# Layer four's attention: the fourth query unit is multiplied before the keys are turned, and its evacuation and squares move with it

## The reference, cut to what matters

```python
z = h @ w_in
cq = rms_norm_2(z[..., :o1], q_norm_g)
ckv = rms_norm_2(z[..., o1:o2], kv_norm_g)
q = (cq @ w_q_up).reshape(b, s, MLA_HEADS, QK_DIM)
kv = (ckv @ w_kv_up).reshape(b, s, MLA_HEADS, NOPE_DIM + V_DIM)
...
q = rms_norm_2(q, qn_g)
k = rms_norm_2(k, kn_g)
q = jnp.concatenate([q[..., :NOPE_DIM], rope(q[..., NOPE_DIM:], positions)], axis=-1)
k = jnp.concatenate([k[..., :NOPE_DIM], rope(k[..., NOPE_DIM:], positions)], axis=-1)
o = causal_block_attention(q, k, v)
...
mem_out = memory_attention(q_mem, mem_k, mem_v, mem_qn_g[i], mem_kn_g[i])
x = x + jnp.concatenate([mix, mem_out], axis=-1) @ w_out
```

## Time and profile before

| what | value |
|---|---|
| median of 3 runs | 1572.5 us (1572.43 to 1573.7) |
| the profiled execution's own time | 1575.78 us |
| its span | 1574.0 us, granted TensorE clock 0.98 on the mean |
| PE, DVE, ACT busy | 95%, 84%, 66% of the span |
| chain that ended last | PE 70%, DVE 20%, ACT 4% of the span |

### The profile page before, as it was taken

How to read it: one execution, slowest core, us unless ns; L and a number is a source line. 1 busy time by engine, 2 the same in 40 slices (tenths; PEclk the granted TensorE clock), 3 DMA queues, 4 the chain that set the end, 5 groups by cost and what they waited for, 6 DMA issues and landing times.

```text
span 1574.0 us, 21212 instructions
## 1 busy us (share of the span) xinstructions
PE 1499.9 (95%) x7150; PEld 1228.4 (78%) x7150; DVE 1316.9 (84%) x1970; ACT 1041.5 (66%) x1523; POOL 104.8 (7%) x204
## 2 busy tenths in 40 slices
PE   8999999979999999989989999999898989999998
PEld 5887877858878778778767888888787778888886
DVE  6778899877878998876678999889886789999897
ACT  4555677745646777648456777777586557787775
POOL 4020000030205000020110000000000000000000
PEclk9999999989999999999989999999999989999999
DMA  9435699974437899853557999999542439999996
GB/s 310 153 116 174 204 340 352 325 228 163 158 121 240 292 347 327 274 193 135 149 161 246 361 357 361 359 338 355 203 138 94 139 101 359 360 359 361 357 333 225
DMA packets 307792, 400.27 MB, mean 254 GB/s; under 512 B 16716, under 2 KB 221260, under 8 KB 307428
## 3 DMA queue, kind: packets, MB, share of 16 engines
q1 hardware_dynamic: 298500, 382.00, 73.1%
q0 software_dynamic: 9184, 16.91, 3.7%
HBM read 397.80 MB, written 1.05 MB: 253 GB/s over the span
## 4 chain that ended last, share of the span: by engine, by line
PE 70%; DVE 20%; ACT 4%; DMA 3%; issue 2%; SPq 0%; DVEq 0%; ACTq 0%; POOLq 0%
PE bank L648 19%; PE bank L649 19%; PE bank L650 19%; DVE w_lo_at L2053 8%; DMA raw_at<-in_moe_w_dram 3%; ACT w_hi_at L1453 1%; PE bank L796 1%; PE bank L665 1%; PE bank L823 1%; PE bank L965 1%; PE bank L770 1%; DVE uc_at L2635 1%; PE bank L771 1%; DVE t_lo_at L2075 1%; ACT probs_a_at L1690 0%
## 5 line engine op out<-in xcount | busy, mean ns | idle before, releaser
L2053 DVE TENSOR_TENSOR w_lo_at<-raw_at,w_hi_at 128x1024 fp32r<-128x1024 f32 (+1 forms) x730 | 853.8, 1213 | 91.4 <-ACT w_hi_at L1453 77.0
L1453 ACT ACTIVATE w_hi_at<-raw_at 128x1024 fp32r<-128x1024 f32 (+1 forms) x730 | 726.2, 1046 | 152.9 <-PE bank L650 69.7
L648 PE MATMUL bank<-w_hi_at,xs_hi_at 128*128 128x512 f32 x800 | 322.7, 403 | 4.0 <-DVE w_lo_at L2053 1.6
L650 PE MATMUL bank<-w_hi_at,xs_lo_at 128*128 128x512 f32 x800 | 313.6, 392 | 0.0
L649 PE MATMUL bank<-w_lo_at,xs_hi_at 128*128 128x512 f32 x800 | 313.5, 392 | 0.0
L648 PE MATMUL bank<-w_hi_at,t_hi_at 128*128 128x512 f32 (+3 forms) x528 | 211.4, 400 | 15.6 <-DVE t_lo_at L2065 7.8
L649 PE MATMUL bank<-w_lo_at,t_hi_at 128*128 128x512 f32 (+3 forms) x528 | 204.1, 387 | 0.0
L650 PE MATMUL bank<-w_hi_at,t_lo_at 128*128 128x512 f32 (+3 forms) x528 | 203.8, 386 | 0.0
L648 PEld LDWEIGHTS bank<-w_hi_at,xs_hi_at 128*128 128x128 f32 x800 | 150.2, 188 | 37.0 <-issue 3.1
L650 PEld LDWEIGHTS bank<-w_hi_at,xs_lo_at 128*128 128x128 f32 x800 | 150.2, 188 | 34.2
L649 PEld LDWEIGHTS bank<-w_lo_at,xs_hi_at 128*128 128x128 f32 x800 | 150.6, 188 | 29.2
(11 more groups left out here) (515 smaller groups left out, 1695.2 us busy)
## 6 DMA issues: line engine op xcount, KB each, us to landing
raw_at<-in_moe_w_dram SPq DMA_DIRECT2D x192, 512.0 KB, 5.7
raw_at<-in_moe_w_gate_dram SPq DMA_DIRECT2D x128, 512.0 KB, 5.7
raw_at<-in_moe_w_up_dram SPq DMA_DIRECT2D x128, 512.0 KB, 7.5
raw_at<-in_moe_w_down_dram SPq DMA_DIRECT2D x128, 512.0 KB, 6.1
raw_at<-in_w_in_dram SPq DMA_DIRECT2D x40, 512.0 KB, 4.9
raw_at<-in_a_w_in_dram SPq DMA_DIRECT2D x20, 512.0 KB, 4.4
raw_at<-in_w_out_dram SPq DMA_DIRECT2D x16, 512.0 KB, 4.2
raw_at<-in_ple_wg_dram SPq DMA_DIRECT2D x16, 512.0 KB, 5.1
```

The lines of the kernel that those rows point to most:

```text
L648: pe.matmul(out, ah, bh, start=start, stop=False, skip_group_check=loose)
L650: return pe.matmul(out, al, bh, start=False, stop=stop, skip_group_check=loose)
L1453: act.activation(WH[:, s.part(), a], RAW[:, s.slot(), a], ACT.Copy).then_inc(hi_half[i], 1)
L2053: dve.tensor_tensor(WL[:, s.part(), a], RAW[:, s.slot(), a], WH[:, s.part(), a].bitcast(F32), ALU.subtract).then_inc(split_half[i], 1)
```

## The change

PE multiplies `unit_q(3)` right behind `unit_q(2)`, ahead of the turn of the keys, instead of behind the query turns. ACT and DVE evacuate it (`query_block(3)`) before the turns, for which the sum of unit 2's squares (`query_squares(2)`) moves ahead too; ACT takes the squares of unit 3 between its `k_rope` evacuation and the split, DVE sums them behind its split as before. The turns and the scores now follow one another with no weight unit between them. No instruction is added or removed, and SP's and POOL's lists are as they were.

```diff
@@ PE
             unit_q(2)
+            unit_q(3)
             turn("k_nope", lambda h: KV[:, :, 256 * h:256 * h + P], 8, [dve_ready.at("k")], low=False, banks=(5, 7, 4, 6))
             mem_values(3, ("heads_m", 3), ATC, (4, 6))
             turn("k_rope", KRP, 4, [], low=False, banks=(5, 7))
...
             turn_queries(0, (5, 7, 4))
-            unit_q(3)
@@ ACT
             query_block(2)
+            query_squares(2)
+            query_block(3)
             turn("k_nope", 8, KTN, banks=(5, 7, 4, 6), scale=GNK[:, 2:3])
             turn(("heads_m", 3), 4, TH[:, 4:8, :], banks=(4, 6))
             turn("k_rope", 4, KTR, banks=(5, 7))
-            query_squares(2)
+            query_squares(3)
             split()
             turn_queries(0, (5, 7, 4))
-            query_block(3)
-            query_squares(3)
             root("q", 16)
@@ DVE
             query_block(2)
+            query_squares(2)
+            query_block(3)
             turn(("heads_m", 3), 4, TH[:, 4:8, :], TL[:, 4:8, :], banks=(4, 6))
-            query_squares(2)
-            split()
-            query_block(3)
+            split()
             query_squares(3)
```

## The result

The changed kernel is slower: 1577.61 us median (20 runs, 1573.98 to 1580.48) against 1572.05 for the kernel before, ratio 1.0037 with a 95% interval of 1.0027 to 1.0047. In 2 of its 20 runs the kernel before took 2882 and 2996 us, and the ratio leaves these out. Two later sets gave 1.0049 (1.0035 to 1.0063) and 1.0026 (1.0012 to 1.0039). The forecast was 1577.3.

A forecast was written before the change was run, and what follows sets the result against it. The prediction took PE as the bound, with 70% of the span in the last-ending chain. Late scores (+2.2 us) and falls of the clock (+2.6) summed to +4.8 on the 1572.5 median: 1577.3 us, range 1572.5 to 1580.0.

The forecast's parts named there:

- `unit_q(3)` into the first gap: PE's wait ahead of the key transposes: the moved unit cuts idle time from 3.7 to 2.1 us, 1.6 saved.
- ACT's three steps ahead of the keys: ACT's keys' evacuation (`ktn`) starts 4.0 us later, so PE idles 3.3 us before `heads_m`.
- The lost cover: Before the first score PE has nothing left while ACT finishes the query evacuations: a second new wait of 2.7 us.
- The sum of the waits: From the units to the first score: waits saved and added make the first score 2.2 us late.
- Behind the scores: PE runs on without a pause and carries the 2.2 us; nothing given back or added, loads cost nothing.
- The clock: PE's clock falls behind both new waits, at `heads_m` and the scores: 1.3 us each, 2.6 in all.
- The total: Whole kernel: +4.8 us, 1577.3 us against the median of 1572.5.
- A: Rival at the new waits: scores late but the clock holds, +2.2 to +3.0 us, central 1574.9; chance 0.31.
- C: Rival from `heads_m` to the scores: the clock stays low over both waits, +2.2 plus 5 to 6, 1580; chance 0.12.
- B: Rival at the keys: gap filled, ACT starts `ktn` by about 1191.7; -2.1, at best about 1570.0 us; chance 0.11.

The follow-up runs named there:

- e5: The changed kernel with 3 added 128x512 matmuls, results unused, in each of PE's two new waits; ratio to the kernel before 1.0029.
- e10: The same kernel as e5, run once more in another set; ratio to the kernel before 1.0014.
- e1: The changed kernel once more, nothing altered, in a later set; 1579.65 us, ratio to the kernel before 1.0049.
- e7: Kernel before, with ACT evacuating memory heads' probabilities ahead of `query_block(1)` and keys ahead of `query_squares(1)` and `query_block(2)`; ratio to before 0.9974.
- e2: The changed kernel, but ACT evacuates the keys ahead of `query_squares(2)` and `query_block(3)`; ratio to the kernel before 1.0013.
- e9: The changed kernel again, nothing altered, in a third set; ratio to the kernel before 1.0026.
- e4: The changed kernel with 5 added 128x512 matmuls, results unused, in each of PE's two new waits; 1578.05 us, ratio to the kernel before 1.0038.

## Why the prediction was right

Measured from the end of `unit_q(2)` (1179.98 in the changed kernel, 1185.33 before):

- *`unit_q(3)` into the first gap:* 2.1 us of wait forecast, 2.29 measured. The 16 key transposes took 1.91 us, against 1.8.
- *ACT's three steps ahead of the keys:* `ktn` 4.0 us later forecast, 4.0 measured; `heads_m` at +11.42 forecast and +11.42 measured; the wait ahead of it 3.3 forecast, 2.94 measured. The 0.4 is in PE's own steps before it.
- *The lost cover:* 2.7 us of wait forecast, 2.86 measured.
- *The sum of the waits:* +2.2 forecast. The first score at full clock came 27.37 - 24.93 = 2.4 us late, and the stretch was 2.5 us longer. `heads_m` at full clock takes 3.53 us, not 3.46. The relay that gives the 2.2 is sound, but the check of it in idle time does not add up as written: `unit_q(3)` lies ahead of the first score in both kernels, so its 4.25 us do not come off. New idle time is 3.3 + 2.7 - 1.6 - 0.4 (small waits) = 4.0 us. Off it go the 0.5 of `heads_m` and a term that the prediction left out, the keys' turn, which ran at the lower clock before (0.63 + 2.64 = 3.27 us) and at the full one after (1.91): 2.1 again. The second part of that turn in the kernel before:

```profile
1189.93 2.64 PE L665 MATMUL bank<-consts_at,kv_at 128*128 128x128 f32 x12 [0.25 <-ACT at_c_at L1817]
```

- *Behind the scores:* nothing given back, nothing added. PE does not wait before L1387 in the changed kernel, and the last 357 us are equal to 0.1 us in the first pair (357.4 to 357.8 us in the three traces of the changed kernel). The first weighed probabilities had 1.9 us to spare by the forecast and 2.4 measured.
- *The clock:* 1.3 for each of two waits, 2.6 in all; the three traces hold 1.4, 4.6 and 1.6, on the mean 2.5. The mean agrees with the forecast, but three draws from 1.4 to 4.6 can do so by luck, and the make-up was wrong: I had a fall behind each wait, each partly hidden. In the traces it differs from one execution to the next. Of the three, two had one behind the first wait and two behind the second (one of these 6.8 us long), and one fell behind the 2.3 us wait that I had priced at nothing. The onset was misread too: read in steps of 0.1 us, the two falls of rows 6 begin 1.1 and 0.8 us behind the end of the wait, not 1.4 and 1.2, and those at the two long waits of the changed kernel from 0.7 us before the end to 0.1 us behind it.
- *The total:* 1577.3 forecast and 1577.6 measured are nearer than the parts. The forecast stands on a median of three runs, 1572.5; against the kernel before the change cost 5.8 us by the ratio (4.2 to 7.4), where 4.8 was forecast and the three stretches give 5.1 on the mean. The kernel before was traced once, so what falls of the clock its other executions hold is open, and with it the rest.

Of the rivals, A (the clock holds) is what e5 and e10 built by hand, at 1.0014 to 1.0029; C has the time of e1 (1580 forecast, 1579.65 measured) but not its mechanism: there the clock was back at 1.00 from 1194.6 to 1201.4, between two falls. B, faster because ACT is out of the way, did not happen by itself, but it named the right condition: e7 brings `ktn` forward and keeps the split covered, and gains what B's best case had, and more.

## What to carry to other kernels

An instruction block that fills one engine's wait is often the cover of another engine's work where it stood; before moving it, write down what the other engines do meanwhile, and what is queued behind the evacuations that move with it. When a trace shows a wait, look for the bank or buffer being freed and at the list of the engine that frees it: here three lines moved on ACT, with PE's order as it was, made the stretch 5 us shorter, where moving PE's block made it 4 to 7 us longer. And where executions of one kernel differ by more than the change is worth, compare the stretch between two fixed instructions, not the spans.

## What the runs showed of the hardware that I had not expected

- A wait of 2.3 us of PE, between two blocks of dense matmuls, had the lower clock begin at its end (e2, 0.4 us before it) or behind it (e9, 1.5 us) in 2 of the 9 traces of kernels that had it unfilled, and not in the other 7.
- A lower-clock stretch behind a wait can be free. In e9 it lengthened `unit_q(3)` by 1.6 us, and the next wait shrank by as much.
- Small float32 matmuls are two records each in the trace: `heads_m` has 8 matmuls and shows 16, and one with 512 columns took 0.86 us in e4, against 0.22 for each of the three rounded products of a weight unit. With 2.6 us of them in each of the long waits the clock was 1.00 in all three traces. (The text ahead of the result counts 16 matmuls in `heads_m`; they are these 16 records.)
- The same instructions ahead of the change took 1172.5 to 1178.7 us in the 14 traces. Of the two shown, of 1173.4 and 1178.7 us, the longer has more of the lower clock (means 0.99 and 0.98). I did not try to steer that.
